# Two weight steps of each pair of heads move from the pair's end to the place in front of the bonus product

## The reference

```python
for i in range(DEPTH):
    h = rms_norm(x, norm_mix_pre[i])
    z = h @ w_in[i]                      # layer 1: also w_in_vres
    # 16 RWKV-7 heads of 64: token shift, then
    #   decay, a, g from small products with decay_w2, iclr_a2, gate_g2
    #   (layer 1: v = v + (v_first - v) * sigmoid(v0 + vd @ v2))
    #   state = state*w + (state @ -kk) (kk*a)^T + v k^T ; y = state @ r, over 256 positions
    #   out = (groupnorm(y) + sum(r * k * r_k) * v) * g        <- the sum is the "bonus"
    # 8 attention heads of 128: rotary, causal softmax(q k^T) v (one block of 256 keys here)
    y = concat([out_rwkv, out_attention]) @ w_out[i]
    x = x + rms_norm(y, norm_mix_post[i])
    h = rms_norm(x, norm_mlp_pre[i])
    x = x + rms_norm(square(relu(h @ w_up[i])) @ w_down[i], norm_mlp_post[i])
```

## Time and profile before

| | |
|---|---|
| time, median of 3 runs | 2846.27 us (2846.05 to 2847.26) |
| the profiled execution's own time | 2847.98 us |
| its span in the trace | 2846.0 us |
| TensorE busy | 2742.3 us, 96% |
| VectorE busy | 1797.4 us, 63% |
| ScalarE busy | 1279.4 us, 45% |
| GpSimd busy | 327.2 us, 11% |
| TensorE waits at L633 for L1223 | 10.2 us, 9 times |
| TensorE waits at L643 for L1250 | 7.8 us, 9 times |

### The profile page before, as it was taken

How to read it: one execution, slowest core, us unless ns; L and a number is a source line. 1 busy time by engine, 2 the same in 40 slices (tenths; PEclk the granted TensorE clock), 3 DMA queues, 4 the chain that set the end, 5 groups by cost and what they waited for, 6 DMA issues and landing times.

```text
span 2846.0 us, 54888 instructions
## 1 busy us (share of the span) xinstructions
PE 2742.3 (96%) x18139; PEld 2277.1 (80%) x18139; DVE 1797.4 (63%) x3008; ACT 1279.4 (45%) x2144; POOL 327.2 (11%) x448
## 2 busy tenths in 40 slices
PE   7999999998999999999989999999989999999997
PEld 6777777786888888888767777777868888888886
DVE  5776666657655556555666666666576565565655
ACT  4443444354444444444444444444544444444443
POOL 2211111112000000000122222221120000000002
PEclk9999999999999999999999999999999999999998
DMA  6333333343566555565533333332535565555553
GB/s 187 98 93 112 98 98 105 99 151 115 183 191 186 184 185 188 181 185 189 153 99 113 98 98 101 95 98 89 179 117 185 186 188 183 183 188 184 184 192 104
DMA packets 518317, 415.98 MB, mean 146 GB/s; under 512 B 19422, under 2 KB 515696, under 8 KB 518256
## 3 DMA queue, kind: packets, MB, share of 16 engines
q1 hardware_dynamic: 515888, 412.88, 47.0%
q0 software_dynamic: 2368, 2.32, 0.3%
HBM read 413.03 MB, written 2.10 MB: 146 GB/s over the span
## 4 chain that ended last, share of the span: by engine, by line
PE 89%; DVE 8%; issue 2%; ACT 1%; DMA 0%; POOL 0%; DVEq 0%; ACTq 0%; POOLq 0%; SPq 0%
PE gemm_bank L537 47%; PE gemm_bank L538 24%; PE gemm_bank L540 3%; PE mix_bank L690 2%; DVE b_yo L1177 1%; PE mix_bank L702 1%; PE mix_bank L699 1%; PE mix_bank L654 1%; DVE b_rn L1209 1%; PE mix_bank L720 1%; PE mix_bank L724 1%; DVE b_yo L1160 1%; PE mix_bank L730 1%; PE mix_bank L734 1%; PE mix_bank L712 1%
## 5 line engine op out<-in xcount | busy, mean ns | idle before, releaser
L537 PE MATMUL gemm_bank<-b_hT,b_whi 128*128 128x512 f32 x3420 | 1273.6, 411 | 29.1 <-DVE b_hT L1157 14.4
L1136 DVE TENSOR_TENSOR b_wlo<-b_raw,b_whi 128x1024 fp32r<-128x1024 f32 x745 | 907.9, 1232 | 497.7 <-ACT b_whi L891 496.4
L891 ACT ACTIVATE b_whi<-b_raw 128x1024 fp32r<-128x1024 f32 x777 | 806.9, 1056 | 488.8 <-PE gemm_bank L538 482.2
L538 PE MATMUL gemm_bank<-b_hT,b_wlo 128*128 128x256 f32 x3648 | 1018.5, 283 | 0.0
L537 PE MATMUL gemm_bank<-b_mT,b_whi 128*128 128x512 f32 x2400 | 856.5, 400 | 1.6 <-DVE b_yo L1142 1.6
L537 PEld LDWEIGHTS gemm_bank<-b_hT,b_whi 128*128 128x128 f32 x3420 | 647.5, 189 | 198.9 <-issue 42.2
L538 PEld LDWEIGHTS gemm_bank<-b_hT,b_wlo 128*128 128x128 f32 x3648 | 695.7, 191 | 14.9 <-issue 5.3
L538 PE MATMUL gemm_bank<-b_mT,b_wlo 128*128 128x256 f32 x2560 | 707.1, 281 | 0.0
L537 PEld LDWEIGHTS gemm_bank<-b_mT,b_whi 128*128 128x128 f32 x2400 | 451.3, 188 | 110.2 <-issue 3.5
L538 PEld LDWEIGHTS gemm_bank<-b_mT,b_wlo 128*128 128x128 f32 x2560 | 484.6, 189 | 7.1
L899 ACT ACTIVATE b_xl<-gemm_bank 128x256 f32<-128x256 f32 x389 | 127.8, 381 | 305.2 <-PE gemm_bank L540 299.7
(11 more groups left out here) (229 smaller groups left out, 2499.4 us busy)
## 6 DMA issues: line engine op xcount, KB each, us to landing
b_raw<-in_w_up SPq DMA_DIRECT2D x256, 512.0 KB
b_raw<-in_w_down SPq DMA_DIRECT2D x256, 512.0 KB
b_raw<-in_w_in SPq DMA_DIRECT2D x384, 256.0 KB
b_raw<-in_w_out SPq DMA_DIRECT2D x48, 512.0 KB
b_raw<-in_w_out SPq DMA_DIRECT2D x32, 256.0 KB
b_raw<-in_w_in SPq DMA_DIRECT2D x8, 512.0 KB
b_yo<-in_x SPq DMA_DIRECT2D x2, 1024.0 KB, 7.9
out<-b_raw SPq DMA_DIRECT2D x8, 256.0 KB, 2.0
```

The source lines that it names most:

```text
L537: mm(bank[b0 + b][:, :], whi[r][:, cols], pair, start=first, stop=False)
L538: m = mm(bank[b0 + b][:, 0:SEQ], wlo[r][:, cols], act[:, kt, 0, :], start=False, stop=False)
L891: f(whi[r][:, :], raw[r][:, :, :].rearrange("p a b -> p (a b)"), ACT.Copy).then_inc(hi_done, 1)
L1136: tt(wlo[r][:, :], flat(raw[r][:, :, :]), whi[r][:, :].bitcast(F32), ALU.subtract).then_inc(lo_done, 1)
```

## The change

In the tensor block's `mixer` the call in front of the bonus product asks for nine steps in place of seven:

```diff
@@ -625,7 +625,7 @@
                 if l:
                     mm(mb[3][:, 0:SEQ], lw[0:VRES, 2, :], lact[0:VRES, 2, :], start=True,
                        stop=True).then_inc(e["lora_v"], 1)
-                fill(7)
+                fill(9)
 
                 pe.wait_ge(e["t1_ready"], V)
                 if l:
```

## The result

The changed kernel took 2889.59 us, the kernel before 2846.77 us beside it, ratio 1.0150 (1.0132 to 1.0167). It is slower, as forecast, but by 42.8 us and not by 18.6. The span of the profiled execution grew from 2846.0 to 2886.7 us, by 40.7.

What follows compares the result with a forecast made beforehand. TensorE, 89% of the chain, was taken as the bound. Layer 0 pairs +5.2, +1.0 and +1.8, layer 1 +8.7 and +1.9, together +18.6 us, gave a median of 2864.9 us, +0.65%, range 2851 to 2872.

Steps and rivals of the forecast that it cites:

- Part 1: Before bonus product L633: two steps, 1.4 us, fill layer 0's 1.46 us wait, nothing gained or lost there yet.
- Part 2: Before L643: slot 3's first step waits for VectorE's split, delaying L643 by 1.53 us in layer 0, 1.92 in layer 1.
- Part 4: Pair's end: two steps less save 1.40 us, but slot 11's first step waits 0.73, so 0.67 us is given back.
- Part 3: From L643 to L775: same instructions run 1.5 to 1.9 us later, no new wait, costed at nothing.
- the gain: Rival: slot 3's first step doesn't wait and TensorE's waits are simply filled; 2830 to 2841 us, chance 0.08.
- the second: Rival: L1223's collision with GpSimd's copies goes, VectorE's queue shortens to 10.90 us in pairs 1 to 6; 2860.8 us, chance 0.14.
- the third: Rival, a draw: L1223's collision goes and nothing waits at slot 11's first step; about +3.5 us, 2849.8 us, chance 0.08.
- The fourth: Rival: VectorE's queue slides into GpSimd's work, one more instruction per loop pair pays 0.83 us; +11.6, 2876.5 us, chance 0.08.

Runs made afterwards that it cites:

- e8: Changed kernel with the bonus product run four times more, same operands and result, just in front of the first weight step of slot 3; 2877.05 us.
- e11: Changed kernel with no weight-slot split on GpSimd, VectorE doing those of slots 1 and 2 instead; 2872.65 us.
- e7: Kernel before the change, with GpSimd's second split of a pair (slot 2) held until VectorE's L1212 is done; 2875.54 us.
- e3: Changed kernel with GpSimd's second split of a pair (slot 2) held until VectorE's L1212 is done; 2905.10 us.

## Why the prediction was right in sign and wrong in size

Two steps of the prediction failed: the clock was costed at nothing, and VectorE's queue was taken to last 11.58 us from L1142 to the end of the split of slot 3. The runs showed about 11.6 us for the clock and a queue of 12.32 us.

**Part 1** held in layer 0 only in part: L633 still waits 0.64 us and comes 8.74 us after L622, before 8.18 (336.89 - 328.71), because VectorE's queue is later. **Part 2** held in mechanism: step 12 waits for the split of slot 3, in front of L643, in all pairs. Its size failed. The forecast was +1.53 us at L643 in layer 0, measured +2.34 (13.84 against 11.50). Of the 0.81 us, 0.55 is L1207 (1.33 against 0.78), 0.19 is that L1223's collision stayed (1.32 us; I had taken 11.58 us for the queue on the guess that the copies would meet it differently), and 0.07 is the gap from the split's end to the next matmul plus the step, 0.91 us (348.11 to 349.02) for my 0.84.

The failed step behind this size is the sentence "L1142 follows on the last steps of the pair before (through ScalarE's copy) and keeps its place in the new pair", with all that I let slide with it. L1142 did, 0.61 us after L622. But the next instruction was held by a split whose start is tied elsewhere. I had written that "GpSimd's start is tied to the split of slot 0 and not to the steps", and had drawn only the effect on L1223, whose 1.32 us caught the eye, and not on L1207 and L1212, which had the same sign in the rows: 0.73 to 0.78 and 0.83 to 0.85 us where the first pair has other values for the same lines (0.23 us for L1212, at 75.50). The sum counted 0.67 us given back per loop pair; L1207 takes 0.55 of it away.

**Part 4** is right in mechanism: step 44 starts behind a wait, 332.19 in the changed kernel, 0.15 us after the split (330.82 + 1.22 = 332.04). What is given back was 2.34 - 1.81 = 0.53 us, forecast 0.67. Per pair in layer 0 that is +1.81 for +0.86.

**Layer 1:** forecast +1.92 - 0.67 = +1.25 us per loop pair. The first two had +1.3 and +1.9, the other five +3.4 to +3.5. The sentence "The longest standstill, about 1.5 us, is as long as today's 1.46", from which I costed the clock at nothing, failed. The standstill was 2.26 to 2.28 us in six of the loop pairs, 0.54 of it from L1207 (1.24 us against 0.70), and 2.73 in the last pair, and behind most of these the clock fell to the 1.2 GHz level. e8 shows that the longer pairs are the clock and prices it at about 11.6 us in all. That is the largest single part of the miss.

**Part 3** held in the loop pairs: from L643 on nothing else waits there up to L775. In the last pairs it did not: L767 now waits 1.1 us for ScalarE's copy L1017, since the two steps that stood between are gone. **The last pairs** lost more than forecast; the last pair of layer 1 together with all behind it grew by 5.8 us (917.9 against 912.1) for my 1.9. The clock is a part of it: it fell behind step 12, and it was 0.83 in the stretch 2030 to 2040 us, behind the waits at L767 and L775. I had not looked there.

In the trace, the 40.7 us are: layer 0 loop pairs 11.9, from its last pair to layer 1's first 2.4, layer 1 loop pairs 20.6, its last pair and the rest 5.8. They are 22.1 over the forecast's 18.6. By an estimate from the rows, about 11.6 of these are the clock and about 7.7 the 0.55 us of L1207 in the 14 pairs where it grew; the small rest has terms of both signs. Of the rivals, the gain needed that step 12 doesn't wait, and it does; the second, relief at L1223, is refuted by its 1.32 us in layer 0; the third needed both that and no wait at step 44. The fourth, a further collision, was the right kind of thing at the wrong instruction: "one more instruction of each loop pair pays 0.83 us", in truth 0.55, and I gave it 0.08.

Two things stay open. By the rows L1207 has 3.3 of layer 0's 11.9 us (six pairs of 0.55), but no run takes it away alone: e11 replaced one hold by another, and a kernel with neither was not run. And why the clock fell behind some standstills of 1.95, 2.26 and 2.8 us and not behind others is not shown.

## What to carry to other kernels

When work is moved so that one engine's phase begins earlier, ask of each other engine what its start hangs on, and slide them against each other instruction by instruction: a duration that differs between places for the same line (0.23 and 0.83 us here) can be a wait in disguise, and it grows when its owner comes earlier. A ring of prepared slots is part of the order: a weight step moved forward over a slot boundary needs that slot's preparation moved too. And a standstill is not harmless because there was one like it before: work out its new length, and give a fallen clock a price of its own in the forecast, since the same length (2.26 us here) left the clock full in one pair and not in the next.

## What the runs showed of the hardware that was not expected

VectorE's `tensor_scalar` L1207 on an SBUF tile of 128x256 took 0.28 us alone and otherwise ended 0.15 to 0.16 us after GpSimd's subtraction beside it; the `tensor_scalar` L1218, 0.38 us alone, was stretched so to 2.43 us in e7; `reciprocal` beside the same subtraction kept its 1.75 us.

TensorE's granted clock stayed at 1.00 behind 1.55 us of standstill. Behind 2.26 us it was at 0.50 in five loop pairs of the changed kernel and at 1.00 in one, and in e3 behind 2.8 us at 1.00 in twelve loop pairs and at 0.50 in two. With 1.89 us of repeated products in the gap 0.54 us of standstill were left, the clock kept 1.00 there, and the kernel was 12.5 us faster.
